# State-space output stage in eight rounds, four of them between the last units of the gate projection

## What is computed

```python
proj = h @ w_in[l]
q, k, v, g_ret, u, g_s5 = jnp.split(proj, SPLITS, axis=-1)
...
ret = retention(q, k, v, ret_gn_g[l]).astype(x.dtype) * jax.nn.silu(g_ret)
ssm = s5_branch(u, ...).astype(x.dtype) * jax.nn.silu(g_s5)
x = x + jnp.concatenate([ret, ssm], axis=-1) @ w_out[l]
```

```python
_, _, xr, xi = lax.associative_scan(combine, (a_seq_re, a_seq_im, bu_re, bu_im), axis=1)
y = (jnp.einsum('blgn,gpn->blgp', xr, c_re) - jnp.einsum('blgn,gpn->blgp', xi, c_im))
y = y.reshape(Bsz, L, W) + d * uf
y = jax.nn.gelu(y)
y = y * jax.nn.sigmoid(y @ glu_w + glu_b)
```

## Time and profile before

| | us |
|---|---|
| median of three runs | 2496.24 |
| profiled execution | 2495.95 |
| its span | 2494.1 |
| PE busy | 2403.3 |
| DVE busy | 1448.1 |
| ACT busy | 691.0 |
| POOL busy | 219.9 |

### The profile page before, as it was taken

The page is one execution under the profiler, slowest core; times in us unless marked ns, Lnnn a source line. Parts: engine busy times, 40 slices in busy tenths (PEclk is TensorE's granted clock), DMA queues, the critical chain, the costliest instruction groups (busy, mean ns, idle before and its releaser), DMA issues.

```text
span 2494.1 us, 35429 instructions
## 1 busy us (share of the span) xinstructions
PE 2403.3 (96%) x14874; PEld 2001.6 (80%) x14874; DVE 1448.1 (58%) x2440; ACT 691.0 (28%) x1081; POOL 219.9 (9%) x95
## 2 busy tenths in 40 slices
...
GB/s 228 119 135 168 173 146 98 86 172 175 171 226 215 220 43 212 135 118 68 60 181 78 118 171 74 92 61 116 43 142 181 192 202 211 141 146 135 122 150 92
DMA packets 271761, 350.11 MB, mean 140 GB/s; under 512 B 34449, under 2 KB 167538, under 8 KB 271602
## 3 DMA queue, kind: packets, MB, share of 16 engines
...
...
## 4 chain that ended last, share of the span: by engine, by line
PE 81%; DVE 10%; ACT 3%; DMA 3%; issue 2%; SPq 1%; ACTq 0%; POOL 0%; DVEq 0%; POOLq 0%
PE PS L500 26%; PE PS L503 18%; PE PS L3253 14%; PE PS L3333 9%; PE PS L679 1%; PE PS L1896 1%; PE PS L1876 1%; DMA LAR<-ret_d 1%; DVE W_LO L408 1%; DMA RAW<-in_w_gate_up 1%; PE PS L2463 1%; DVE XN L640 1%; PE PS L2458 1%; PE PS L1161 1%; PE PS L1081 1%
## 5 line engine op out<-in xcount | busy, mean ns | idle before, releaser
L500 PE MATMUL PS<-W_HI,OP_HI 128*128 128x512 f32 (+1 forms) x1152 | 300.5, 404 | 5.3 <-DVE XI L1449 2.9
L500 PE MATMUL PS<-W_LO,OP_HI 128*128 128x512 f32 (+1 forms) x1152 | 282.1, 387 | 0.8 <-DVE W_LO L408 0.8
L500 PE MATMUL PS<-W_HI,OP_LO 128*128 128x512 f32 (+1 forms) x1152 | 279.0, 384 | 0.0
L441 POOL TENSOR_SCALAR W_HI<-RAW 128x2048 fp32r<-128x2048 f32 (+1 forms) x66 | 130.1, 1983 | 1536.9 <-PE PS L500 688.7
L500 PEld LDWEIGHTS PS<-W_HI,OP_HI 128*128 128x128 f32 x1152 | 213.8, 195 | 51.2 <-issue 5.3
L500 PEld LDWEIGHTS PS<-W_LO,OP_HI 128*128 128x128 f32 x1152 | 215.8, 190 | 45.7 <-DVE W_LO L408 1.2
L500 PEld LDWEIGHTS PS<-W_HI,OP_LO 128*128 128x128 f32 x1152 | 212.6, 188 | 42.8 <-issue 0.5
L529 ACT ACTIVATE OST<-PS 128x512 f32<-128x512 f32 (+2 forms) x152 | 85.7, 564 | 471.2 <-PE PS L503 262.6
L408 DVE TENSOR_TENSOR W_LO<-RAW,W_HI 128x2048 fp32r<-128x2048 f32 (+1 forms) x52 | 129.3, 2504 | 106.4 <-POOL W_HI L441 106.3
L503 PE MATMUL PS<-OP_HI,W_HI 128*128 128x512 f32 x704 | 180.2, 398 | 0.0
L503 PE MATMUL PS<-OP_HI,W_LO 128*128 128x512 f32 x704 | 174.7, 390 | 0.0
...
## 6 DMA issues: line engine op xcount, KB each, us to landing
RAW<-in_w_gate_up SPq DMA_DIRECT2D x88, 512.0 KB, 5.7
...
LE<-spill_d SPq DMA_DIRECT2D x22, 512.0 KB, 4.7
...
ptok_d<-OST ACTq DMA_DIRECT2D x24, 256.0 KB, 2.0
```

What stands on the lines that cost most here:

```text
L441: nc.gpsimd.tensor_scalar(hi, raw, 1.0, 1.0, ALU.mult, ALU.mult).then_inc(*w_hi.by(1))
L500: ins = nc.tensor.matmul(PS[:, bank, 0:width], act_part[:, k, a * P:(a + 1) * P], w_part[:, slot, k, 0:width], start=start, stop=stop)
```

## The change

Feed stage: ACT stores each turned tile of u to a new scratch tensor `ut_d` (16 stores of 256 KB), and `UTq` has two buffers.

gs5: the units go by halves of the sequence (eight units of both blocks for the first 512 rows, then eight for the second), so the second block's weights are wanted at unit 4. `LOW_SCAN` does its last two low parts (halves 18 and 19) eight columns earlier. The low parts of halves 20 and 21 go from POOL to DVE.

Output stage: a round loads the kept tiles in two parts m of 256 KB with 256 KB of `CY` each, and `TY` as before; the regrouping, the turning of u and the copy to `UTy` are gone. The rounds 0 to 3 stand in front of gs5's units 12 to 15, the rounds 4 to 7 behind them in a row, with the results of rounds 4 and 6 in the banks 0 and 1. ACT evicts units 12 and 13 between Gelu of round 1 and round 2, and units 14 and 15 behind round 7. Gelu goes in two halves of the sequence; the high parts of the second half come behind unit 15's eviction, their low parts on DVE behind the first half's. The low parts of halves 22 and 23 stand last in DVE's list of the stage, and POOL makes their high parts only when the first half of y is complete. glu's units of the second half wait for the second half of y.

```diff
+    def halves_in_turn(g):
+        g.units.sort(key=lambda u: u[2])
+        for b in {u[0] for u in g.units}:
+            last = max(n for n, u in enumerate(g.units) if u[0] == b)
+            blocks[b] = (blocks[b][0], g.first + last + 1)
...
+    halves_in_turn(gemms["gs5"])
...
-    DVE_HALVES = tuple(range(20))
+    DVE_HALVES = tuple(range(22))
...
+            if b == gemms["glu"].first_block + 1 and half == 0:
+                pool.wait_ge(*la_lo(KT))
...
+            if h and second_half:
+                pe.wait_ge(*second_half)
+                second_half = None
...
-            yield n + 0.9
+            yield times.get(n, n + 0.9)
...
-            if m:
-                act.wait_ge(*s5b_mm(m))
-            act.activation(UTq[:, :, :].rearrange("p g n -> p (g n)"), PS[:, 4 + m % 2, :], ACT.Copy)\
+            if m >= 2:
+                act.wait_ge(*s5b_mm(m - 1))
+                act.wait_ge(*ut_out[m % 2](16 * (m // 2)))
+            act.activation(UTq[m % 2][:, :, :].rearrange("p g n -> p (g n)"), PS[:, 4 + m % 2, :], ACT.Copy)\
                .then_inc(*s5b_ut.by(1))
+            act.wait_ge(*s5b_ut(m + 1))
+            act.dma_start(ut_d[:, m, :], UTq[m % 2][:, :, :].rearrange("p g n -> p (g n)")).then_inc(*ut_out[m % 2].by(16))
...
-    LOW_SCAN = {12: 14, 16: 15, 56: 16, 60: 17, 100: 18, 104: 19}
+    LOW_SCAN = {12: 14, 16: 15, 56: 16, 60: 17, 92: 18, 96: 19}
...
+    BESIDE = 4
+    Y_START = 11.95
...
+    def y_banks(q):
+        return 0 if q >= BESIDE and q % 2 == 0 else 4
...
+    def sp_y_part(sp, m):
+        if m >= 2:
+            sp.wait_ge(*s5y_mm(m - 1))
+        sp.dma_start(UT2[m % 2][:, :, :].rearrange("p g n -> p (g n)"), ut_d[:, m, :]).then_inc(*s5y_u[m % 2].by(16))
+        sp.dma_start(CY2[m % 2][:, :, :, :], cc_d[:, 2 * m:2 * m + 2, :, :]).then_inc(*s5y_u[m % 2].by(16))
...
+    def sp_y_next(sp, parts):
+        for m in parts:
+            sp_y_part(sp, m)
+            if m % 2 and m + 1 < PARTS and m >= 3:
+                sp_y_toeplitz(sp, (m + 1) // 2)
...
+        def products(q):
+            first = y_banks(q)
+            if q == 0:
+                pe.wait_ge(*scan_step(SCAN_END))
+            elif q < BESIDE:
+                pe.wait_ge(*s5y_ys(2 * q))
+            elif q == BESIDE:
+                pe.wait_ge(*bank_act(gemms["gs5"].free0_act + 14))
+            else:
+                pe.wait_ge(*s5y_ys(2 * q - 2))
+            pe.wait_ge(*s5y_in[q % 2](16 * (q // 2 + 1)))
+            place = lambda g: PS[:, first + g % 2, (g // 2) * P:(g // 2 + 1) * P]
+            for m in (2 * q, 2 * q + 1):
+                pe.wait_ge(*s5y_u[m % 2](32 * (m // 2 + 1)))
+                groups = range(4 * (m % 2), 4 * (m % 2) + 4)
+                for g in groups:
+                    T.matmul(place(g), UT2[m % 2][:, g % 4, :], TY2[q % 2][:, :, 16 * g:16 * g + 16], start=g < 2, stop=False)
+                for c in range(2):
+                    for g in groups:
+                        lo = 64 * (g % 2)
+                        ins = T.matmul(place(g), SCAN[lo:lo + 64, c, 4 * q + g // 2, 0:NCH],
+                                       CY2[m % 2][lo:lo + 64, g // 2 % 2, c, :], start=False, stop=c == 1 and g >= 6)
+                ins.then_inc(*s5y_mm.by(1))
...
+        for q in range(BESIDE):
+            yield Y_START + q
+            products(q)
+            yield Y_START + q + 0.95
+            turn_back(q)
+        products(BESIDE)
+        for q in range(BESIDE, 8):
+            if q + 1 < 8:
+                products(q + 1)
+            turn_back(q)
...
+            yield Y_START + q + 1.2
+            act.wait_ge(*s5y_tt(q + 1))
+            for h in range(2):
+                act.activation(y_value(q, h).rearrange("c (n i) -> c n i", i=SC),
+                               PS_T(6)[:, :, 64 * h:64 * h + 64].rearrange("c i n -> c n i"),
+                               ACT.Gelu_apprx_tanh).then_inc(*s5y_yo.by(1))
+            act_y_high(act, q, 0)
+        yield Y_START + 20
+        for q in range(8):
+            act_y_high(act, q, 1)
...
-        regroup(0)
-        for _ in dve_split_later(dve, "glu", (0, 1), skip=2):
-            continue
+        first_glu = 2 * gemms["glu"].first_block
         for q in range(8):
-            if q + 1 < 8:
-                regroup(q + 1)
-            dve.wait_ge(*s5y_mm(q + 1))
+            dve.wait_ge(*s5y_mm(2 * q + 2))
             if q:
                 dve.wait_ge(*s5y_tt(q))
             for par in range(2):
                 nc.vector.tensor_copy(YS[:, :, par::2, :].rearrange("n i g c -> n g i c"),
-                                      PS[:, 4 + par, :].rearrange("n (g i c) -> n g i c", g=4, i=SC))\
+                                      PS[:, y_banks(q) + par, :].rearrange("n (g i c) -> n g i c", g=4, i=SC))\
                     .then_inc(*s5y_ys.by(1))
+            if q < 2:
+                dve_low_part(dve, first_glu + q)
             if q:
-                dve_y_low(dve, q - 1)
-        dve_y_low(dve, 7)
+                dve_y_low(dve, q - 1, 0)
+        dve_y_low(dve, 7, 0)
+        for q in range(8):
+            dve_y_low(dve, q, 1)
+        for _ in dve_split_later(dve, "glu", (0, 1), skip=2):
+            continue
...
-            sp_s5_y(sp, range(1))
+            sp_y_first(sp)
+            sp_weights(sp, weights_before("gs5"))
+            sp_y_next(sp, range(2, 6))
             sp_weights(sp, weights_before("glu") - 2)
-            wait_stores(sp, "gs5")
-            sp_s5_y(sp, range(1, 8))
-            sp_weights(sp, weights_before("glu"))
+            sp_y_next(sp, range(6, PARTS))
+            wait_stores(sp, "gs5", more=-4)
...
-            act_gemm_store(act, "gs5", ch_to(gs5_d), func=ACT.Silu)
-            act_s5_y(act)
+            together(act_gemm_store_steps(act, "gs5", ch_to(gs5_d), func=ACT.Silu,
+                                          times={12: 14.5, 13: 14.51, 14: 30.0, 15: 30.1}), act_s5_y(act))
...
-            pe_gemm(pe, "gs5")
-            pe_s5_y(pe)
-            together(one_after_other(pe_gemm_steps(pe, "glu", ready=[(la_lo, KT - 1)], last_tile=la_lo(KT)), 2 * TT,
-                                     pe_gemm_steps(pe, "out_s5", operand=(la_lo, KT))), pe_retention(pe))
+            together(pe_gemm_steps(pe, "gs5"), pe_s5_y(pe))```

On PE, around what was the end of gs5's unit 11: before, the last units follow each other and the stage begins behind the last one.

```order
L503 MATMUL PS<-OP_HI,W_HI 128x512 [waits bank_act]
L503 MATMUL PS<-OP_HI,W_HI 128x512 x7
L503 MATMUL PS<-OP_HI,W_LO 128x512 x8
L503 MATMUL PS<-OP_LO,W_HI 128x512 x8
L1272 MATMUL PS<-CONST,URy 128x128 [waits s5y_ur,bank_act,scan_step]
L1272 MATMUL PS<-CONST,URy 128x128 x7
L1282 MATMUL PS<-TYa,UTy 128x128 [waits s5y_in0,s5y_ut]
L1282 MATMUL PS<-TYa,UTy 128x128 x7
L1286 MATMUL PS<-CYa,SCAN 128x128 x16
```

More of the change, by code:

```diff
@@ L514, in act_gemm_store, with act_gemm_store_steps @@
         alone(act_gemm_store_steps(act, name, dst, func, gain))
-    def act_gemm_store_steps(act, name, dst, func=ACT.Copy, gain=None, silu={}):
+    def act_gemm_store_steps(act, name, dst, func=ACT.Copy, gain=None, silu={}, times={}):
         g = gemms[name]
         for n, (b, a, h, width) in enumerate(g.units):
-            yield n + 0.9
+            yield times.get(n, n + 0.9)
             s = stores[0]
@@ L1231, in build @@
[L1231 to L1251 removed]
+    UT2 = (at("UTa", "extra", 8192, [P, 4, P]), at("UTb", "extra", 10240, [P, 4, P]))
@@ new lines, in build @@
+    TY2 = (at("TYa", "extra", 0, [P, SC, P]), at("TYb", "extra", 4096, [P, SC, P]))
+    CY2 = (at("CYa", "extra", 12288, [P, 2, 2, P]), at("CYb", "stage", 8192, [P, 2, 2, P]))
+    YS = at("YS", "stage", 10240, [P, SC, 8, SP_])
+    YL = at("YL", "oplo", 0, [P, KT, L])
+    YB2 = tuple(at(f"YB{q}", "stage", 14336 + 2048 * q, [P, HALF]) for q in range(3))
+    s5y_u = (sem("s5y_u0"), sem("s5y_u1"))
+    s5y_in = (sem("s5y_in0"), sem("s5y_in1"))
+    s5y_mm, s5y_ys, s5y_tt, s5y_yo = (sem(n) for n in ("s5y_mm", "s5y_ys", "s5y_tt", "s5y_yo"))
@@ new lines, in build, with y_value, sp_y_toeplitz @@
+    BESIDE = 4
+    Y_START = 11.95
+    def y_banks(q):
+        return 0 if q >= BESIDE and q % 2 == 0 else 4
+    def y_value(q, h):
+        return YB2[q][:, :] if h and q < len(YB2) else YL[:, q, h * HALF:(h + 1) * HALF]
+    def sp_y_toeplitz(sp, q):
+        if q >= 2:
+            sp.wait_ge(*s5y_mm(2 * q - 2))
+        sp.dma_start(TY2[q % 2][:, :, :], toep_d[:, :, q * P:(q + 1) * P]).then_inc(*s5y_in[q % 2].by(16))
+    def sp_y_part(sp, m):
[3 more added lines that the diff above has]
+        sp.dma_start(CY2[m % 2][:, :, :, :], cc_d[:, 2 * m:2 * m + 2, :, :]).then_inc(*s5y_u[m % 2].by(16))
@@ new lines, in sp_y_first @@
+    def sp_y_first(sp):
+        sp.wait_ge(*s5_zero_out(16 * (SC - 1)))
+        sp.wait_ge(*s5_out(S5_STORES))
+        sp.wait_ge(*s5b_mm(PARTS))
+        sp.wait_ge(*s5_r(NSL))
+        for done in ut_out:
+            sp.wait_ge(*done(16 * PARTS // 2))
+        for q in range(2):
```

(21 more changed lines are left out.)

98 lines of the change are left out of this document (17 added, 81 removed), and 10 rows, old and new, of the table SHARED.

## The result

The changed kernel took 2496.97 us (median of 18 runs, 2490.81 to 2504.53), the kernel before, on the same chip, 2491.97 us (18 runs, 2487.81 to 2497.75). The ratio is 1.0020, 95% interval 1.0012 to 1.0029: some 5 us slower, inside what I called no change, and inside the range. The profiled execution of the changed kernel took 2492.95 us with a span of 2491.2, which is *less* than the 2495.95 of the one before, so the two executions can't be compared from their starts.

What follows compares the result with a forecast made beforehand. Kernel time was taken to follow DVE's arrival at MEMSET RST: PE leaves the stage 8.9 us earlier, DVE arrives 3.5 us later. 2495.95 + 3.5 = 2499.5, said as 2500, range 2490 to 2507.

Steps and rivals of the forecast that it cites:

- Part 1: Feed stage and gs5: stores cost 0, PE waits 0.8 us at unit 4, round 0 starts at 512.4.
- Part 2: Rounds 0 to 3 beside gs5 units: 4 x (3.86 + 5.45 + 0.93) = 41.0 us, to 553.4.
- Part 3: Rounds 4 to 7: part loads limit; the last turning ends at 579.7, PE leaving the stage 8.9 us earlier.
- L: Output stage: time from the signal freeing a part's buffer to the landing of both its DMAs, taken as 4.2 us.
- B: End of the output stage's last turning back on PE, forecast as 567.1 + 3L = 579.7.
- Rival 3: Rounds 5 to 7: part loads take 6.3 us, giving 2505.8, or 2511 with PE's clock fallen; chance 0.13.
- Part 4: DVE's work before serving retention's first turning: MEMSET RST at 596.8, 3.5 us later than before.
- The clock: Behind PE's wait at retention's first turning: same 3.0 us loss as before, so change 0, between -2 and +3.
- The sum: Whole kernel: 2495.95 + 3.5 = 2499.5, said as 2500.
- Rival 1: Behind the output stage: the gain passes through, 8.7 us at glu's start stay, 2487.3; chance 0.10.
- Rival 2: Output stage: loads don't limit (L = 3.1) and Gelu reads fast, 1.6 us less, giving 2494.6; chance 0.18.
- Rival 4: ACT's table load behind the last turning: the page's drain adds 1.4 us, giving 2501; chance 0.04.

Runs made afterwards that it cites:

- rounds behind: All eight output rounds placed behind gs5's last unit, otherwise as the changed kernel: 0.0066, 16.5 us, slower than the changed kernel.
- both repairs: The same run as e7: 0.9947 of the kernel before, 18 us faster than the changed kernel.
- POOL early: Changed kernel with only POOL's wait for the first half of y, before splitting halves 22 and 23, removed: 1.0027 of the kernel before.
- The third buffer: Changed kernel with a third buffer for the parts from part 10 on: 0.0004, 1 us, under the changed kernel.
- the last pair of runs: Changed kernel without POOL's wait for y's first half: with evictions of units 14 and 15 last, 2.3 us under the changed kernel; alone, 1.0027 of the kernel before.
- e3: Changed kernel with weights' low parts in rounds 5 and 6, y's second-half low parts behind retention's preparation: 0.0042, 10.5 us, under the changed kernel.
- e5: e3 with ACT making the second half's eight high parts behind retention's sine and cosine: 0.0014, 3.5 us, under e3.
- e7: e5 with a third buffer for the parts from part 10 on: 0.9947 of the kernel before, 18 us faster than the changed kernel.

## Why the prediction was right

The mechanism was the one forecast: PE leaves earlier, DVE arrives later, and the time follows DVE. Over all runs the shift at the attention against the kernel before and the measured ratio agree to 2 us: changed +5.2 and +5.0; rounds behind +19.6 and +21.4; both repairs -11.5 and -13.2; the worst, POOL early, +4.7 and +6.7.

That 5.2 and 5.0 agree to a fraction is luck: the interval of the ratio is 3 to 7 us, and a column of the table is good to about 3.

**Part 1.** PE's wait at unit 4 was 0.3 us, not 0.8, and round 0 began 65.9 us behind gs5's start (66.15 predicted). The scan had ended some 13 us before it.

**Part 2.** Right in kind, 1.8 us too small: four rounds took 42.8 instead of 41.0. The term that was mis-sized is the products, 4.25 instead of 3.86: L1306 and L1310 now stand in four blocks a round, one pair for each part, where they stood in two. The unit behind them takes 5.58, not 5.45, and the turning back 0.87, not 0.93. That the changes from block to block cost the time is likely, but was not tested by itself.

**Part 3.** Waits for parts limit the tail, as said. From the signal to the first product L was 3.7, 4.1 and 5.7 for parts 10, 12 and 14, 13.5 together where I took 12.6. With the longer products B came 27.96 us behind the tail's start, not 26.3. The third buffer shows the reason. One wait had the wrong owner: the last turning stood behind the copy to `YS` (1.45 us), not behind round 6's Gelu, which ended 0.3 us sooner. Rival 3's 6.3 did not come, though part 14 came near; its clock did not fall, 1.00 in the window.

**Part 4.** From B to MEMSET RST 15.56 instead of 17.1. Gelu was the term mis-sized: 1.09 for two halves, not 2.06, and less than the lower end of 1.26 that I had named. The POOL term was too large here (0.5 instead of 0.7), because ACT kept DVE waiting past most of it; the last pair of runs shows that it was a cover for another delay and not small by nature. The rest held: table load 1.28, the first second-half high part started at B + 5.0 (5.8 less the 1.0 of Gelu), two weight parts 4.48, and 9.93 to the turning. PE's wait was 14.44 (15.8).

**The clock.** From the turning to the scores the changed kernel took 9.36 us against 9.34: the same loss, as taken.

**The sum.** +3.3 at B and -1.5 behind it make MEMSET RST 5.2 us later than before, where I had 3.5; measured +5.0. The two mis-sized terms partly cancelled. The median of 2497 against my 2500 owes some of its nearness to the chip: there the kernel before ran at 2492, 4 us under the median I started from.

**The rivals.** Rival 1, the gain passes through, fell, but it is what the order decides: with the list changed (e3, e5, e7) it came, and more. Rival 2 had Gelu right and the loads wrong. Rival 4: the table load at 578.92 is followed by the next activation at 580.22, 0.02 behind its end. The Trainium skill (ScalarE: Activation LUTs, What ACT_TABLE_LOAD costs) has a drain of about the load's length at each switch; this trace, like the one before, shows none. The Trainium skill (SBUF — State Buffer, the note on cachelines) says of a non-contiguous access to PSUM that it slows matmuls; that it would slow ACT's read too was my extension of it. The extension is not borne out: 0.60 for 512 columns, the time of the contiguous rows.
